# Scale weights in two halves, and the scale of chunks 4 to 7 computed inside the opening unit

## The reference

```python
mod_lat = (jax.nn.silu(c) @ w_mod[layer] + b_mod[layer])[:, None, :]
mod_ctx = (jax.nn.silu(c_ctx) @ w_mod[layer] + b_mod[layer])[None, None, :]
x  = x  + 0.5 * ml[2] * swiglu(rms_norm(x)  * (1 + ml[1]) + ml[0], ffn1_w_in, ffn1_w_out)
cx = cx + 0.5 * mc[2] * swiglu(rms_norm(cx) * (1 + mc[1]) + mc[0], ffn1_w_in, ffn1_w_out)
```

## Time and profile before

| | us |
|---|---|
| median of 3 runs | 1251.53 |
| lowest, highest | 1251.45, 1252.37 |
| the profiled execution | 1253.0 |
| its span | 1250.9 |
| TensorE busy in the span | 1235.6 |
| scale's last quarter landed | 22.3 |
| unit 0's first matmul | 28.42 |

### The profile page before, as it was taken

The page is one execution under the profiler, slowest core; times in us unless marked ns, Lnnn a source line. Parts: engine busy times, 40 slices in busy tenths (PEclk is TensorE's granted clock), DMA queues, the critical chain, the costliest instruction groups (busy, mean ns, idle before and its releaser), DMA issues.

```text
span 1250.9 us, 20691 instructions
## 1 busy us (share of the span) xinstructions
PE 1235.6 (99%) x7800; PEld 1090.3 (87%) x7800; DVE 892.2 (71%) x1400; ACT 580.4 (46%) x898; POOL 55.7 (4%) x65
## 2 busy tenths in 40 slices
PE   8999999999999999999999999999999999999998
PEld 6788888888888899988999888889999999888887
DVE  3887777778757665777666676667869977667765
ACT  3532222321326446644444654546465566554553
POOL 2000000000002000100001000000001301000001
PEclk8999999999999999999999999999999999999999
DMA  9565544555412244432445465554643335455542
GB/s 389 222 243 202 202 166 172 200 202 202 149 62 93 104 166 139 164 101 102 168 168 202 151 245 176 195 178 164 228 144 105 132 113 190 167 174 206 193 168 101
DMA packets 31827, 214.22 MB, mean 171 GB/s; under 512 B 3473, under 2 KB 4753, under 8 KB 7057
## 3 DMA queue, kind: packets, MB, share of 16 engines
q1 hardware_dynamic: 31184, 211.83, 46.7%
q10 hardware_dynamic: 576, 1.48, 0.3%
HBM read 212.24 MB, written 1.05 MB: 171 GB/s over the span
## 4 chain that ended last, share of the span: by engine, by line
PE 95%; DVE 2%; DMA 1%; issue 1%; ACT 0%; SPq 0%; DVEq 0%
PE ps_u L1915 20%; PE ps_u L1916 19%; PE ps_u L1917 19%; PE ps_u L1906 18%; PE ps_u L1908 9%; DMA scr<-in_mods 1%; PE ps_a L1830 1%; PE ps_a L2132 1%; PE ps_a L2117 1%; PE ps_a L1887 1%; PE ps_a L2321 1%; PE ps_a L1842 0%; PE ps_a L1876 0%; PE ps_u L1979 0%; PE ps_a L1865 0%
## 5 line engine op out<-in xcount | busy, mean ns | idle before, releaser
L536 ACT ACTIVATE w_hi<-raw 128x1024 fp32r<-128x1024 f32 x322 | 338.8, 1056 | 308.4 <-PE ps_u L1917 191.2
L1052 DVE TENSOR_TENSOR w_lo<-raw,w_hi 128x1024 fp32r<-128x1024 f32 x322 | 394.3, 1226 | 107.5 <-ACT w_hi L536 107.0
L1915 PE MATMUL ps_u<-x_hi,w_hi 128*128 128x256 f32 (+1 forms) x1136 | 370.8, 326 | 0.0
L1917 PE MATMUL ps_u<-x_hi,w_lo 128*128 128x256 f32 (+1 forms) x1136 | 362.1, 319 | 0.0
L1916 PE MATMUL ps_u<-x_lo,w_hi 128*128 128x256 f32 (+1 forms) x1072 | 344.2, 321 | 0.0
L1915 PEld LDWEIGHTS ps_u<-x_hi,w_hi 128*128 128x128 f32 x1136 | 216.2, 190 | 21.4 <-issue 6.2
L1917 PEld LDWEIGHTS ps_u<-x_hi,w_lo 128*128 128x128 f32 x1136 | 216.1, 190 | 15.3
L1916 PEld LDWEIGHTS ps_u<-x_lo,w_hi 128*128 128x128 f32 x1072 | 204.1, 190 | 15.3 <-issue 0.5
L1915 PE MATMUL ps_u<-h_hi,w_hi 128*128 128x256 f32 (+1 forms) x432 | 141.7, 328 | 0.4 <-DVE h_hi L1296 0.4
L1917 PE MATMUL ps_u<-h_hi,w_lo 128*128 128x256 f32 (+1 forms) x432 | 140.9, 326 | 0.0
L1916 PE MATMUL ps_u<-h_lo,w_hi 128*128 128x256 f32 (+1 forms) x368 | 122.9, 334 | 0.0
(11 more groups left out here) (313 smaller groups left out, 1399.4 us busy)
## 6 DMA issues: line engine op xcount, KB each, us to landing
raw<-in_stream SPq DMA_DIRECT2D x153, 1024.0 KB, 4.8
wide_scr<-in_mods SPq DMA_DIRECT2D x18, 1024.0 KB, 7.0
scr<-in_mods SPq DMA_DIRECT2D x18, 1024.0 KB, 7.0
raw<-in_stream SPq DMA_DIRECT2D x8, 768.0 KB, 4.2
x<-in_tokens SPq DMA_DIRECT2D x2, 1024.0 KB, 6.4
wide_scr<-in_cmp_w SPq DMA_DIRECT2D x8, 256.0 KB, 5.1
sq<-in_cmp_w SPq DMA_DIRECT2D x2, 1024.0 KB, 8.0
out<-x SPq DMA_DIRECT2D x4, 256.0 KB, 2.2
```

The costliest lines, as they stand in the source:

```text
L536: act.activation(w_hi[:, k % 2, cols], raw[:, k % 2, cols], ACT.Copy).then_inc(h_ready, 1)
L1052: dve.tensor_tensor(w_lo[:, k % 2, cols], raw[:, k % 2, cols], w_hi[:, k % 2, cols].bitcast(F32), ALU.subtract).then_inc(l_ready, 1)
L1915: pe.matmul(dst, wh, xh, start=(kc == 0), stop=False)
L1917: ins = pe.matmul(dst, wl, xh, start=False, stop=(kc == span - 1))
```

## The change

The host lays out the four scale quarters so that output channels 0 to 511 stand in the first half of each row and 512 to 1023 in the second. SP loads the four first halves (512 KiB each), then unit 0's weights, then the four second halves. The shift's quarters 4 to 7 wait for the second halves to be multiplied (`mod_done` of 5 to 8), where they waited for quarters 0 to 3. TensorE multiplies a half quarter with `scale_mod`: as many matmul calls as a quarter, 128 columns in place of 256. First halves go ahead of unit 0; all four second halves ahead of its kc 1. VectorE computes the scale of chunks 0 to 3 before the first z, and that of chunks 4 to 7 (`scale_half(1)`) after `x_lo` of chunk 3, ahead of z of chunk 4. The shift's quarters are multiplied ahead of kc 4, 5 and 6 (two there), `times_shift` moves behind unit 0, the copy of its rows from behind `lo(3)` to behind `lo(1)`, and the sum from unit 1's kc 2 to kc 4. The filler of four matmul calls is gone, that of nine follows the spread. The other edits only raise the counts of waits by one.

```diff
+            def scale_load(h, q):
+                cols = slice(h * MOD_HALF, (h + 1) * MOD_HALF)
+                sp.dma_start(mod_slots[q][:, cols], a["mods"][q, :, cols]).then_inc((half_landed if h else mod_landed)[q], LANDED)
-            for u in range(4):
-                if u == 3:
-                    load(0, 0, KD)
-                mod_load(u, u)
+            for q in range(MOD_QUARTERS):
+                scale_load(0, q)
+            load(0, 0, KD)
+            for q in range(MOD_QUARTERS):
+                scale_load(1, q)
             for u in range(4, MOD_FRONT):
-                sp.wait_ge(mod_done, u - 3)
+                sp.wait_ge(mod_done, MOD_QUARTERS + u - 3)
                 mod_load(u, u - 4)
...
+            def scale_half(h):
+                part, cols = slice(4 * h, 4 * h + 4), slice(KD + 4 * h, KD + 4 * h + 4)
+                dve.wait_ge(mod_done, MOD_QUARTERS * (h + 1))
+                dve.transpose(turned[:, h * P:(h + 1) * P], ps_a[:, h, 0:P]).then_inc(mod_turned, 1)
...
                     if between is None:
+                        if kc + 1 < KD:
+                            z(kc + 1)
                         lo(kc)
                     else:
+                        if kc not in (3, KD - 1):
+                            z(kc + 1)
                         scaled(kc)
                         if kc == 2:
                             split(0, 0, 1)
+                        if kc == 3:
+                            scale_half(1)
+                            z(kc + 1)
...
                         lo(kc)
-                        if kc == 3:
+                        if kc == 1:
                             dve.wait_ge(shift_rows, 1)
...
                                 unit(0, base, from_x(n), n, ready=scaled)
+                                pe.wait_ge(shift_ready, 1)
+                                times_shift(0, ps_a[:, 3, 0:S]).then_inc(shift_rows, 1)
...
+            def scale_mod(h, q):
+                pe.wait_ge((half_landed if h else mod_landed)[q], LANDED)
+                for kc in range(2):
+                    for g in range(P // MOD_ROWS):
+                        lo = h * MOD_HALF + (kc * (P // MOD_ROWS) + g) * P
+                        ins = pe.matmul(ps_a[g * MOD_ROWS:(g + 1) * MOD_ROWS, h, 0:P], sc_pad[:, 2 * q + kc, :], mod_slots[q][:, lo:lo + P],
+                                        start=(q == 0 and kc == 0), stop=(q == MOD_QUARTERS - 1 and kc == 1))
+                ins.then_inc(mod_done, 1)
-            front_mod(0)
+            scale_mod(0, 0)
             stat_rows(0, 4, range(SUMMED, KD), SUMMED, 0)
-            front_mod(1)
+            scale_mod(0, 1)
             stat_rows(0, 4, (0,), SUMMED, 0)
-            front_mod(2)
+            scale_mod(0, 2)
+            scale_mod(0, 3)
             spread(0, 4)
-            keep_busy_front(4)
-            front_mod(3)
             keep_busy_front(9)
             def scaled(kc):
-                if 1 <= kc <= MOD_QUARTERS:
-                    front_mod(MOD_QUARTERS + kc - 1)
+                if kc == 1:
+                    for q in range(MOD_QUARTERS):
+                        scale_mod(1, q)
+                if 4 <= kc <= 6:
+                    front_mod(kc)
+                if kc == 6:
+                    front_mod(KD - 1)
                 pe.wait_ge(scaled_lo, kc + 1)
-                if kc == 6:
-                    pe.wait_ge(shift_ready, 1)
-                    times_shift(0, ps_a[:, 3, 0:S]).then_inc(shift_rows, 1)
...
             def normed_and_summed(kc):
-                if kc == 2:
+                if kc == 4:
                     pe.wait_ge(shift_copied, 1)
```

More of the change, by code:

```diff
@@ L38 @@
 MOD_FRONT = 2 * MOD_QUARTERS
+MOD_HALF = KD * P
 MOD_RIDE = N_MOD * MOD_QUARTERS - MOD_FRONT
@@ L263, in program @@
         xl_ready = sem("x_lo_ready")
+        half_landed = [sem(f"second_half_of_scale_landed{i}") for i in range(4)]
         scaled_hi = sem("unshifted_x_hi_ready")
@@ L416, in riding_load @@
                 if n < 4:
-                    sp.wait_ge(mod_done, MOD_FRONT + n - 3)
+                    sp.wait_ge(mod_done, MOD_FRONT + n + 1)
                 else:
@@ L627, in _ @@
             splits(0, 1)
-            act.wait_ge(mods_ready, 2)
+            act.wait_ge(mods_ready, 3)
             norm_hi(0, NB, 0)
@@ L642, in kv_parts @@
                 if i == 0:
-                    act.wait_ge(scale_ready, 2)
+                    act.wait_ge(scale_ready, 3)
                 if i == 1:
@@ L1090, in modulation @@
                 if c < 2:
-                    dve.wait_ge(mod_done, MOD_QUARTERS * (c + 1))
+                    dve.wait_ge(mod_done, MOD_QUARTERS * (c + 2))
                 else:
@@ L1094, in modulation @@
                 dve.transpose(turned[:], ps_a[:, b, 0:MOD_COLS]).then_inc(mod_turned, 1)
-                dve.wait_ge(mod_turned, c + 1)
+                dve.wait_ge(mod_turned, c + 2)
                 cols = slice(chunk * KD, (chunk + 1) * KD)
@@ L1098, in modulation @@
                    .then_inc(mods_ready, 1)
-                dve.wait_ge(mods_ready, c + 1)
+                dve.wait_ge(mods_ready, c + 2)
+            def scale_half(h):
+                part, cols = slice(4 * h, 4 * h + 4), slice(KD + 4 * h, KD + 4 * h + 4)
+                dve.wait_ge(mod_done, MOD_QUARTERS * (h + 1))
+                dve.transpose(turned[:, h * P:(h + 1) * P], ps_a[:, h, 0:P]).then_inc(mod_turned, 1)
+                dve.wait_ge(mod_turned, h + 1)
+                dve.tensor_tensor(mods[:, cols, :], turned_cols[:, part, :], bm[:, cols].unsqueeze(2).broadcast_to([P, 4, 2]), ALU.add)\
+                   .then_inc(mods_ready, 1)
+                dve.wait_ge(mods_ready, h + 1)
+                dve.scalar_tensor_tensor(am[:, 0, part, :], mods[:, cols, :], 1.0,
+                                         vec[:, V_N1 + 4 * h:V_N1 + 4 * h + 4].unsqueeze(2).broadcast_to([P, 4, 2]), ALU.add, ALU.mult)\
+                   .then_inc(scale_ready, 1)
+                dve.wait_ge(scale_ready, h + 1)
             def scale_of(i, chunk, v):
@@ L1143, in norm_lo @@
                 for kc in range(KD):
-                    if kc + 1 < KD:
-                        z(kc + 1)
                     if between is None:
+                        if kc + 1 < KD:
+                            z(kc + 1)
                         lo(kc)
                     else:
+                        if kc not in (3, KD - 1):
+                            z(kc + 1)
                         scaled(kc)
@@ L1253, in _ @@
             split(0, 0, 0)
-            modulation(0, 1, 0)
-            scale_of(0, 1, V_N1)
-            dve.wait_ge(scale_ready, 1)
+            scale_half(0)
             def shift():
-                modulation(1, 0, 1)
+                modulation(1, 0, 0)
                 dve.tensor_copy(shift_pad[:, :, 0:2], mods[:, 0:KD, :]).then_inc(shift_ready, 1)
@@ L1319, in swiglu @@
                                         split(0, FIRST["k"] - 2, 0)
-                                        dve.wait_ge(scale_ready, 2)
+                                        dve.wait_ge(scale_ready, 3)
                                         dve.tensor_copy(shift_pad[:, :, 0:2], mods[:, 3 * KD:4 * KD, :]).then_inc(shift_ready, 1)
@@ L1356, in _ @@
             k = FIRST["k"]
-            dve.wait_ge(scale_ready, 3)
+            dve.wait_ge(scale_ready, 4)
             dve.wait_ge(gate_ready, 2)
@@ L1882, in mod_sum @@
                 pe.wait_ge(mod_added, 4 * MOD_QUARTERS * (c + 1))
-                pe.wait_ge(mod_turned, c if c >= 3 else 2)
+                pe.wait_ge(mod_turned, c + 1 if c >= 3 else 3)
                 for v in range(2):
@@ L1986, in front_mod @@
             def front_mod(u):
-                mod(u, u // MOD_QUARTERS, u % MOD_QUARTERS, u % 4, LANDED * (u // 4 + 1), 0)
-            front_mod(0)
+                if u == MOD_QUARTERS:
+                    pe.wait_ge(mod_turned, 1)
+                mod(u, 0, u % MOD_QUARTERS, u % 4, LANDED * 2, 0)
+            def scale_mod(h, q):
[7 more added lines that the diff above has]
+            scale_mod(0, 0)
             stat_rows(0, 4, range(SUMMED, KD), SUMMED, 0)
-            front_mod(1)
+            scale_mod(0, 1)
             stat_rows(0, 4, (0,), SUMMED, 0)
-            front_mod(2)
+            scale_mod(0, 2)
+            scale_mod(0, 3)
             spread(0, 4)
-            keep_busy_front(4)
-            front_mod(3)
             keep_busy_front(9)
             def scaled(kc):
-                if 1 <= kc <= MOD_QUARTERS:
-                    front_mod(MOD_QUARTERS + kc - 1)
+                if kc == 1:
[5 more added lines that the diff above has]
+                    front_mod(KD - 1)
                 pe.wait_ge(scaled_lo, kc + 1)
-                if kc == 6:
-                    pe.wait_ge(shift_ready, 1)
-                    times_shift(0, ps_a[:, 3, 0:S]).then_inc(shift_rows, 1)
             def times_shift(k, dst):
@@ L2025, in _ @@
             pe.wait_ge(cst_landed, 16)
```

(4 more changed lines are left out.)

## The result

| | before | after |
|---|---|---|
| median, us | 1251.49 (6 runs) | 1256.09 (6 runs) |
| lowest, highest | 1251.04, 1252.37 | 1254.36, 1257.69 |
| ratio, 95% interval | | 1.0035, 1.0025 to 1.0046 |
| profiled execution, span | 1253.0, 1250.9 | 1255.55, 1253.4 |

In later runs the unedited kernels came out at 1251.63 and 1255.51. The two profiles differ by 2.5 us of span, the medians by 4.6. A second profile of the kernel before, at 1251.68, has a span of 1249.7; against that one, the changed kernel's 1253.4 is 3.7 us longer.

The account below looks back on a forecast made before the run. TensorE was taken to bound the kernel, busy 1235.6 of 1250.9 us. Unit 1 starting at 44.15 in place of 45.73, counted as 1.5 us and subtracted from the median of 1251.53, gave 1250.0; range 1248.2 to 1252.6.

Parts of the forecast that it names:

- third part of the forecast: Shift's loads and unit 1's weights: weights land at 39.85, 5 us later; unit 1 starts at 44.15, 1.6 us early.
- 0.9 us to spare: End of unit 1: it ends at 55.5, unit 2's first hidden chunk is needed at 54.6, so it fits.
- I took 0.6: Unit 0: TensorE time for one second half quarter, 0.6 us; four add 2.4 us.
- 62 ns: Half quarters: per-MATMUL sequencer time from the skill; by it a half costs 1.0 us and the gain is 1.1 us.
- first part: Opening: unit 0's weights come as the fifth MiB, so its first matmul is at 22.4, 6.0 us earlier.
- I take 17.0: Opening: landing of unit 0's weights, at 17.0 us, with 16.15 and 17.9 as ends.
- second rival: Starved queue: late weights and slower load steps start unit 1 at 46.45 or later; 1252.3 to 1254.2 us; chance 0.13.
- a low clock: Rival: half clock around unit 0's start, kc 0 takes 1.3 us more, no gain; 1251.8 us; chance 0.22.
- TensorE idle for about 1 us: Sign expected in the changed profile: a new TensorE pause behind times_shift, released by VectorE, about 1 us.
- Raised counts cost nothing: Waits throughout: the raised wait counts were priced at nothing.
- the gain goes on: After unit 1: unit 2 does not wait for its hidden chunk, so the 1.5 us counted at unit 1 is kept.
- the mark of unit 1: Start of unit 1, 45.73 us before: the change is worth what it moves this, if what follows keeps up.

Follow-up runs that it names:

- e10: Changed kernel with its fillers in matmul calls of 512 columns (10 in place of 31, 2 in place of 9): 1253.18 us.
- e11: e10 with two more filler calls of 512 columns in the pause ahead of unit 1: 1252.91 us.
- e12: e2 with the short program (fillers in calls of 512 columns): 1251.06 us.
- e13: Kernel before, with its fillers in calls of 512 columns, 112 instructions shorter: 1253.60 us.
- e6: e4 with its fillers in calls of 512 columns (10 in place of 31, 2 in place of 9): 1249.25 us.
- e2: Changed kernel with unit 1's weights issued ahead of the shift's four quarters instead of behind them: 1252.62 us.
- e4: Changed kernel with the half quarters packed by pairs into 1 MiB loads with full rows: 1250.49 us.
- e5: Changed kernel again, unedited, for a second profile: 1255.51 us.
- e3: Changed kernel with seven narrow filler matmul calls behind times_shift, in the pause ahead of unit 1: 1255.10 us.

## Why the prediction was wrong

**Right.** The third part of the forecast is the mechanism: the shift's loads behind TensorE, the queues empty, unit 1's weights late, TensorE held behind `times_shift` with `x_lo` as releaser. Its intervals held. From unit 0's first matmul to the issue of quarter 4: 2.25 forecast, 25.84 - 23.61 = 2.23. Five MiB from there: 15.2 forecast, 15.4. From the landing to unit 1: 4.3 forecast, 4.46. Unit 2 did not wait for its hidden chunk. (The forecast's sum there has a slip: 44.15 + 7 x 0.81 + 0.42 is 50.2, not 49.9, so 0.3 of the 0.9 us to spare was not there; unit 2 did not need it.) Four second halves cost 1.93 us, 0.48 each, where I took 0.6. That is 30 ns for each of 64 instructions, so the 62 ns of the Trainium skill's "Wait — 56ns, not 53.3ns?" (TensorE: Matmul & The Clock Gate) did not bind here, though sixteen in 1.00 us agreed with it in the earlier trace rows; a half quarter, with half the columns, cost half of that quarter's 1.00.

**Wrong, first part: "I take 17.0".** Unit 0's weights landed at 18.15, beyond my upper end of 17.9. The step from 16.15 to 19.86 in the earlier trace rows was in front of me: I put it down to the stream's loads being slow. An instruction load starts at 14 to 15 in both kernels; in e10, e11 and e12, where it starts at 19, the weights land at 16.9 to 17.0, and in e13 at 18.8 in place of 19.85. Rows of half the length are not the reason, since e10 has them too; they may cost up to 0.8 us, for in e6, with full rows, the same fifth MiB is in at 16.1 (issued at 2.87, landed 13.2 us later). The 1.15 us go through every later interval of the changed kernel's profile, as the second rival said, to unit 1: 44.15 forecast, 45.68 measured, of which 0.4 are the sum of small terms. The term alone was not decisive: e10 had it right and still started unit 1 at 45.27.

**Wrong, the clock.** I gave a low clock 0.22 and looked for it in front of unit 0. The pause that I forecast behind `times_shift`, about 1 us, was 1.88 us long and had another of 1.11 us ahead of it; the granted clock fell at 46.4, inside unit 1, and cost 1.9 us. I listed the pause among the signs and priced only its length, not the clock behind it. This is the step that failed with the largest price in the profile: "TensorE idle for about 1 us" stood in the forecast, and what follows it stood in the sum at nothing.

**Wrong, nothing afterwards.** "Raised counts cost nothing" and "the gain goes on" left out that with 28 calls more the instruction loads start at other moments. Near 865 that cost 0.8 us (0.8 to 1.5 over five profiles). "Raised by one" in the part on the change is also short: the waits on `mod_done` of the shift's and the riding quarters rise by four, since the scale now takes eight products. TensorE's timeline has no pause between 24 and 62 us but the two named, so this cost nothing there.

**The base.** The profiled execution of before was 1.5 us slower than its median. Of this, 1.1 stand at unit 1 against its second profile: its own opening had 6.8 us of low clock. I took the difference off as a constant. The second profile, 1251.68 and so near the median, had 3.4 us of it, and the opening that the change removes had less to give: 44.6 and not 45.7 as the mark of unit 1. Against that mark the forecast itself would have been a gain of 0.4, not 1.5.

Together: 1.1 at unit 1, 1.9 for the clock, 0.8 near 865 make the 3.75 us between the profile of the changed kernel and the second of before; the medians differ by 3.8 to 4.6. By the timed runs, the place of unit 1's weights in the order costs the changed kernel 2.9 us (e2) or, with the short program, 2.1 (e12 against e10). The narrow fillers, and with them the moments of the instruction loads, cost it 2.3 to 2.9 (e10), of which the profiles place 1.25. The two shares may overlap, since both bear on how often the clock falls. What the reordering costs by itself, with the effect of the instruction loads taken out, stays open: 1.2 us more by e10 against before, 0.4 less by e10 against e13.

## What to carry to other kernels

A load that is moved behind a wait on the engine it feeds takes all loads behind it in the queue along: e12 against e10, one line's order, is 2.1 us. Before splitting a transfer to start earlier, see that slots come free as early as before; packing halves by pairs kept the early start and freed two slots (e4, e6). A pause is to be priced with the clock behind it. And when a change adds or removes instructions, look at the instruction queue's line beside the landing of every load that the bounding engine waits for: in e6 and e10 the same computation with wider fillers was 1.2 and 2.3 to 2.9 us faster, in e13 1.9 us slower.

## What the runs showed of the hardware

A 16 KB instruction load (queue q8) beside a weight load goes with a landing 0.8 to 1.5 us later: 4.0 to 4.3 us without, 5.1 to 5.5 with, for 768 KB near 865, with one exception (e13: 4.2 with it); 5.6 for 1 MiB near 1077 against the usual 4.8; 16.9 against 18.15 us for unit 0's weights. Its row shows 6 to 7% of 16 engines over 1 us in the opening, and 5.9% over 2 us in the changed kernel near 865; worked out from these, it holds one of the 16 engines for about 1 to 1.9 us. That this is how the delay comes about is an inference from those shares and was not tried by itself. In the opening of the changed kernel the first three of these loads start at 14, 26 and 39.

A pause of 1.8 to 1.9 us on TensorE, with one of 0.9 to 1.4 us some 5 us ahead of it, was followed by the low clock in the profiles of the changed kernel (46.4 to 49.8, and 47.9 to 51.3 in e5) and of e10. With the second pause filled (e3, e11) or taken away (e2, e12) the clock stayed full there. That it falls in some executions of one kernel and not in others is likely from the times and was not profiled: e10's runs split six to five, 1.2 us apart.
